# Attention's value products over four query tiles instead of two

## What is computed

```python
def attend(qblk):
    sc = jnp.einsum('bqkgd,bskd->bkgqs', qblk, k).astype(jnp.float32) * scale
    p = jax.nn.softmax(sc, axis=-1).astype(v.dtype)
    return jnp.einsum('bkgqs,bskd->bqkgd', p, v)
# y_b = attention * silu(g_b);  y = concat([y_a, y_b]);  out = y @ w_out
```

## Time and profile before

| | |
|---|---|
| median of 3 runs | 2314.97 us (2313.32 to 2316.97) |
| the profiled execution | 2311.51 us, of which the span of the trace is 2309.7 us |
| PE busy | 2269.6 us, 98% of the span |
| PEld busy | 1921.3 us, 83% |
| DVE busy | 1077.2 us, 47% |
| ACT busy | 888.3 us, 38% |
| POOL busy | 274.0 us, 12% |
| DMA | 61 GB/s over the span |
| granted tensor clock | 0.999 of full speed |

### The profile page before, as it was taken

The page is one execution under the profiler, slowest core; times in us unless marked ns, Lnnn a source line. Parts: engine busy times, 40 slices in busy tenths (PEclk is TensorE's granted clock), DMA queues, the critical chain, the costliest instruction groups (busy, mean ns, idle before and its releaser), DMA issues.

```text
span 2309.7 us, 28550 instructions
## 1 busy us (share of the span) xinstructions
PE 2269.6 (98%) x11640; PEld 1921.3 (83%) x11640; DVE 1077.2 (47%) x1439; ACT 888.3 (38%) x1426; POOL 274.0 (12%) x276
## 2 busy tenths in 40 slices
PE   7999999999999999999999999998999999999998
PEld 7887799988988779998788898887888888888887
DVE  4323399954433259983624252326344344342343
ACT  5122477744322257773434142323222222222232
POOL 0097200000029600000013020000000000000000
PEclk9999999999999999999999999999999999999999
DMA  6111000033311000003411101322111111124232
GB/s 202 37 55 37 1 1 1 1 137 111 92 55 55 18 1 1 1 8 121 146 60 37 64 19 37 111 73 85 53 54 47 43 54 43 47 95 150 92 127 73
DMA packets 104210, 141.48 MB, mean 61 GB/s; under 512 B 11670, under 2 KB 65094, under 8 KB 104102
## 3 DMA queue, kind: packets, MB, share of 16 engines
q1 hardware_dynamic: 104102, 139.97, 18.3%
HBM read 123.18 MB, written 16.78 MB: 61 GB/s over the span
## 4 chain that ended last, share of the span: by engine, by line
PE 94%; DVE 3%; ACT 1%; issue 1%; DMA 0%; SPq 0%; DVEq 0%; ACTq 0%
PE ps L199 24%; PE ps L201 24%; PE ps L200 24%; PE ps L970 5%; PE ps L985 3%; PE ps L986 3%; PE ps L957 2%; PE ps L958 2%; PE ps L934 1%; PE ps L228 1%; PE ps L275 1%; PE ps L921 1%; PE ps L1949 1%; PE ps L671 1%; DVE hT_lo L290 1%
## 5 line engine op out<-in xcount | busy, mean ns | idle before, releaser
L199 PE MATMUL ps<-w_hi,hT_hi 128*128 128x512 f32 (+1 forms) x1760 | 678.9, 386 | 1.8 <-DVE hT_lo L238 1.4
L201 PE MATMUL ps<-w_hi,hT_lo 128*128 128x512 f32 (+1 forms) x1760 | 672.7, 382 | 0.0
L200 PE MATMUL ps<-w_lo,hT_hi 128*128 128x512 f32 (+1 forms) x1760 | 672.3, 382 | 0.0
L183 DVE TENSOR_TENSOR w_lo<-w_raw,w_hi 128x2048 fp32r<-128x2048 f32 x89 | 207.7, 2334 | 542.1 <-ACT w_hi L167 539.6
L199 PEld LDWEIGHTS ps<-w_hi,hT_hi 128*128 128x128 f32 x1760 | 332.0, 189 | 65.7 <-DVE hT_lo L238 1.9
L201 PEld LDWEIGHTS ps<-w_hi,hT_lo 128*128 128x128 f32 x1760 | 331.9, 189 | 64.3
L200 PEld LDWEIGHTS ps<-w_lo,hT_hi 128*128 128x128 f32 x1760 | 332.0, 189 | 62.6 <-issue 0.5
L199 PE MATMUL ps<-hT_hi,w_hi 128*128 128x512 f32 x832 | 324.2, 390 | 5.0 <-DVE X L2519 2.7
L167 ACT ACTIVATE w_hi<-w_raw 128x2048 fp32r<-128x2048 f32 x71 | 135.9, 1914 | 502.2 <-PE ps L201 502.2
L201 PE MATMUL ps<-hT_hi,w_lo 128*128 128x512 f32 x832 | 323.7, 389 | 0.0
L200 PE MATMUL ps<-hT_lo,w_hi 128*128 128x512 f32 x832 | 323.7, 389 | 0.0
(11 more groups left out here) (203 smaller groups left out, 2365.0 us busy)
## 6 DMA issues: line engine op xcount, KB each, us to landing
w_raw<-in_ffn_w_up SPq DMA_DIRECT2D x44, 512.0 KB, 4.8
w_raw<-in_ffn_w_down SPq DMA_DIRECT2D x22, 1024.0 KB, 4.9
w_raw<-in_w_in SPq DMA_DIRECT2D x21, 1024.0 KB, 5.1
x_mid<-X SPq DMA_DIRECT2D x24, 512.0 KB, 2.7
w_raw<-in_gla_w_in SPq DMA_DIRECT2D x12, 1024.0 KB, 5.2
X<-in_x SPq DMA_DIRECT2D x16, 512.0 KB, 6.9
w_raw<-in_w_out SPq DMA_DIRECT2D x8, 1024.0 KB, 7.0
X<-x_mid SPq DMA_DIRECT2D x16, 512.0 KB, 7.2
```

The lines of the kernel that those rows point to most:

```text
L183: engine.tensor_tensor(self.p.w_lo[:, slot, 0:size], self.p.w_raw[:, slot, 0:size], plane(self.p.w_hi[:, slot, 0:size]), ALU.subtract).the ...
L199: nc.tensor.matmul(out, a_hi, b_hi, start=first, stop=False)
L200: nc.tensor.matmul(out, a_hi, b_lo, start=False, stop=False)
L201: return nc.tensor.matmul(out, a_lo, b_hi, start=False, stop=last)
```

## The change

A constant `QUAD = 4` takes the place of the group size 2.

- `values` works on groups of four items: 512 columns in a matmul, and a group's 16 matmuls are spread over four iterations, four in each. Two groups of four items are kept, so `PT_hi` and `PT_lo` double in size and now cover the whole of `hT_hi` and `hT_lo`.
- Values of group g are made in iterations 4g+6 to 4g+9 (before, of a group of two, 2g+4 and 2g+5). The first value product thus comes two iterations later, and the last one two iterations later.
- `OT` holds 512 columns, and is copied every fourth iteration (n mod 4 = 1); `turn_o` turns four tiles back, every fourth iteration (n mod 4 = 3), starting at 11. DVE's line 1146 then works on four tiles in that iteration.
- The turns of `ya` move from iterations 64 to 67 to iterations 66 to 69.

```diff
-        self.PT_hi = prog.at("PT_hi", [P, 2, TT, 2 * P], 16, F32R)
-        self.PT_lo = prog.at("PT_lo", [P, 2, TT, 2 * P], 48, F32R)
+        self.PT_hi = prog.at("PT_hi", [P, 2, TT, QUAD * P], 0, F32R)
+        self.PT_lo = prog.at("PT_lo", [P, 2, TT, QUAD * P], 32, F32R)
...
-        for j in range(2):
+        for j in range(QUAD):
             mm = self.p.nc.tensor.matmul(self.out_cols(g, j), self.OT[:, g % 2, j * P:(j + 1) * P],
                                          self.pair_ident[:], start=True, stop=True)
...
-                pe.wait_ge(self.pt_lo, 4 * g + 4)
-            for k in range(part * (TT // 2), (part + 1) * (TT // 2)):
+                pe.wait_ge(self.pt_lo, 2 * QUAD * (g + 1))
+            for k in range(part * (TT // QUAD), (part + 1) * (TT // QUAD)):
                 v = self.VS[:, head // (H_B // KV), k, :]
-                nc.tensor.matmul(prog.ps[:, 7, 0:256], v, self.PT_hi[:, g % 2, k, :], start=(k == 0), stop=False)
-                mm = nc.tensor.matmul(prog.ps[:, 7, 0:256], v, self.PT_lo[:, g % 2, k, :], start=False,
+                nc.tensor.matmul(prog.ps[:, 7, :], v, self.PT_hi[:, g % 2, k, :], start=(k == 0), stop=False)
+                mm = nc.tensor.matmul(prog.ps[:, 7, :], v, self.PT_lo[:, g % 2, k, :], start=False,
                                       stop=(k == TT - 1))
-            if part == 1:
+            if part == QUAD - 1:
                 mm.then_inc(self.ot_ready, 1)
...
-            if n % 2 == 1 and 7 <= n < NT + 5:
-                self.turn_o(pe, (n - 7) // 2, n)
-            if 4 <= n < NT + 4:
-                values(n // 2 - 2, n % 2)
-            if NT <= n < NT + 4:
-                if n == NT:
+            if n % QUAD == 3 and 11 <= n < NT + 7:
+                self.turn_o(pe, (n - 11) // QUAD, n)
+            if 6 <= n < NT + 6:
+                values((n - 6) // QUAD, (n - 6) % QUAD)
+            if NT + 2 <= n < NT + 6:
+                if n == NT + 2:
                     pe.wait_ge(self.inp.ga_used, TT)
                     pe.wait_ge(self.exp_done, NT)
-                for g in range(2 * (n - NT), 2 * (n - NT) + 2):
+                for g in range(2 * (n - NT - 2), 2 * (n - NT - 2) + 2):
                     self.ya.pe(pe, g, ya_src)
             if self.turns_head(n):
-                self.turn_head(pe, KV + n // TT + 1, n % TT // 4, max(0, (n - 6) // 2))
+                self.turn_head(pe, KV + n // TT + 1, n % TT // 4, max(0, (n - 7) // QUAD))
...
-            if n % 2 == 1 and 5 <= n < NT + 5:
-                g = (n - 5) // 2
+            if n % QUAD == 1 and 9 <= n < NT + 9:
+                g = (n - 9) // QUAD
                 act.wait_ge(self.ot_ready, g + 1)
...
-            if n % 2 == 1 and n >= 7:
-                g = (n - 7) // 2
+            if n % QUAD == 3 and n >= 11:
+                g = (n - 11) // QUAD
                 dve.wait_ge(self.o_ready, g + 1)
-                dve.wait_ge(self.inv_done, 2 * g + 2)
-                for j in range(2):
-                    m = 2 * g + j
+                dve.wait_ge(self.inv_done, QUAD * (g + 1))
+                for j in range(QUAD):
+                    m = QUAD * g + j
```

More of the change, by code:

```diff
@@ L830, in pool @@
                                     ).then_inc(self.ga_used, 1)
+QUAD = 4
 class Attention:
@@ L850, in __init__ @@
         self.pair_ident = prog.at("pair_ident", [P, HD], kb + 92.75)
-        self.PT_hi = prog.at("PT_hi", [P, 2, TT, 2 * P], 16, F32R)
-        self.PT_lo = prog.at("PT_lo", [P, 2, TT, 2 * P], 48, F32R)
+        self.PT_hi = prog.at("PT_hi", [P, 2, TT, QUAD * P], 0, F32R)
+        self.PT_lo = prog.at("PT_lo", [P, 2, TT, QUAD * P], 32, F32R)
         self.PR = [prog.at(f"PR{i}", [P, SEQ], kb_) for i, kb_ in
                    enumerate((64 + other, 68 + other, 80 + other))]
-        self.OT = prog.at("OT", [P, 2, 2 * P], 84 + other)
+        self.OT = prog.at("OT", [P, 2, QUAD * P], 84 + other)
         self.VS = prog.at("VS", [P, KV, TT, P], 96 + other, F32R)
@@ L890, in pt_of @@
     def pt_of(self, PT, m, half):
-        return PT[:, m // 2 % 2, 4 * half:4 * half + 4, m % 2 * P:(m % 2 + 1) * P]
+        return PT[:, m // QUAD % 2, 4 * half:4 * half + 4, m % QUAD * P:(m % QUAD + 1) * P]
     def out_cols(self, g, j):
-        c = g % 2 * P + j * HD
+        c = g % 2 * QUAD * HD + j * HD
         return self.p.ps[:, 6, c:c + HD]
@@ L918, in turn_head @@
         if outs:
-            pe.wait_ge(self.o_done, 2 * outs)
+            pe.wait_ge(self.o_done, QUAD * outs)
         for j in range(4):
@@ L928, in turn_o @@
         if g >= 1:
-            pe.wait_ge(self.o_done, 2 * g)
+            pe.wait_ge(self.o_done, QUAD * g)
         pe.wait_ge(self.lo_done, 2 * (KV + 1) + sum(self.turns_head(m) for m in range(n)))
@@ L938, in last_output @@
     def last_output(self, pe):
-        self.turn_o(pe, self.NT // 2 - 1, self.NT + 5)
+        self.turn_o(pe, self.NT // QUAD - 1, self.NT + 7)
     def pe(self, pe):
@@ L974, in values @@
         def values(g, part):
-            head = 2 * g // TT
+            head = QUAD * g // TT
             if part == 0:
@@ L1040, in act @@
                 m = n - 2
-                if m >= 4 and m % 2 == 0:
-                    act.wait_ge(self.ot_ready, m // 2 - 1)
+                if m >= 2 * QUAD and m % QUAD == 0:
+                    act.wait_ge(self.ot_ready, m // QUAD - 1)
                 for half in range(2):
@@ L1062, in act @@
                     act.wait_ge(self.o_ready, g - 1)
-                nc.scalar.activation(self.OT[:, g % 2, :], prog.ps[:, 7, 0:256], ACT.Copy).then_inc(self.ot_taken, 1)
-            if NT <= n < NT + 4:
-                for g in range(2 * (n - NT), 2 * (n - NT) + 2):
+                nc.scalar.activation(self.OT[:, g % 2, :], prog.ps[:, 7, :], ACT.Copy).then_inc(self.ot_taken, 1)
+            if NT + 2 <= n < NT + 6:
+                for g in range(2 * (n - NT - 2), 2 * (n - NT - 2) + 2):
                     self.ya.act(act, g)
@@ L1112, in dve @@
         QKV, G = self.inp.QKV, self.inp.G
-        for n in range(NT + 6):
+        for n in range(NT + 8):
             if self.turns_head(n - 1):
@@ L1126, in dve @@
                 m = n - 2
-                if m >= 4 and m % 2 == 0:
-                    dve.wait_ge(self.ot_ready, m // 2 - 1)
+                if m >= 2 * QUAD and m % QUAD == 0:
+                    dve.wait_ge(self.ot_ready, m // QUAD - 1)
                 for half in range(2):
```

## The result

| | before | after |
|---|---|---|
| median of 22 runs | 2314.82 us | 2318.59 us (2316.51 to 2319.84) |
| ratio, after to before | | 1.0014, 95% interval 1.0008 to 1.0021 |
| the profiled execution | 2311.51 us, span 2309.7 | 2316.51 us, span 2314.8 |

The change costs 3.2 us by the ratio (1.9 to 4.9 by its interval), 3.8 by the medians. I had said -3.3, and a range to 2318 us; the time is 0.6 us above it. The change is as small as forecast, about 0.2%, but it has the other sign, and the sum was wrong by about 6.5 us.

A forecast was written before the change was run, and what follows sets the result against it. PE was taken to bound the kernel (94% of the chain), with DVE close behind in attention. The terms -3.8 - 2.2 - 3.4 + 1.4 + 4.2 + 0.5 gave -3.3 us, from 2315.0 to 2311.7 us, range 2306 to 2318.

The forecast's parts named there:

- values of 512 columns: Value products on PE: halving the matmul count saves 0.03 us a block over 128 blocks, -3.8 us.
- turned back by fours: PE's turn-back of outputs: eight instructions in a row cost 0.81 us instead of 0.88, 32 times, -2.2 us.
- wait in iteration 5 goes: Turn-back in iteration 5 of a head no longer waits for DVE's q_lo: 7 heads, 2 layers, -3.4 us.
- new wait in iteration 6: PE's transposes in iteration 6 of a head wait about 0.1 us for DVE's low parts, 14 times, +1.4 us.
- start: Two value blocks leave iterations 4 and 5, where PE waits anyway, and are paid at the end: +4.2 us.
- end: End of attention: PE waits some 0.5 us in iterations 65 and 66, older waits go; net +0.5 us.
- The reading that idle time of the first iterations belongs to DVE: First iterations of attention: PE waits for DVE's low parts, so work removed there saves nothing; behind the +4.2 us.
- The isolated formula: Value matmuls: columns over 2.4 GHz plus about 2.5 ns each, an alternative saving of 1.3 us instead of 3.8.
- The slower one: Rival: DVE takes over behind every turned head, low parts 0.5 to 0.7 us late, 2320 us; chance 0.12.
- The faster one: Rival: value products run at the wide projection's 0.227 us and no new stall appears, 2307.5 us; chance 0.32.
- The sustained 131 ns at 512 columns: Rival that stationary loads set the value matmuls' distance: 0.52 us for four, -64 us; chance 0.01, inside faster.

The follow-up runs named there:

- q_twos: The changed kernel, values still 512 columns wide, but each group's four outputs turned back two at a time in every odd iteration; 2316.85 us, ratio 1.0015 to the kernel before.
- q_heads: The changed kernel with the second half of each next head turned in iteration 6 instead of 4; 2316.81 us, ratio 1.0011 to the kernel before.
- p_lag2: The kernel before, still groups of two, but four groups kept and values, turn-back and ya two iterations later; 2319.95 us, ratio 1.0023.

## Why the prediction was wrong, point by point

| term, both layers | forecast | measured | from |
|---|---|---|---|
| values of 512 columns | -3.8 | -3.7 | q_twos against before, 0.029 x 128 |
| turned back by fours | -2.2 | 0 | q_twos against after, 0.45 and -0.44 |
| wait in iteration 5 goes | -3.4 | -2.9 | 12 x 0.24, distance in 5 |
| new wait in iteration 6 | +1.4 | +3.2 | 12 x 0.27, q_twos and q_heads |
| start | +4.2 | +4.2 | first values, p_lag2 |
| end | +0.5 | +2.1 | the rest of 2 x 1.46; the starts at the end give 2.2 |
| sum | -3.3 | +2.9 | attentions of both layers |

Two terms were right to 0.1 us: the width, and the start, which was the largest. The old wait had the right size, 0.24 us, and the wrong count: I read 28 entries as seven heads with two waits in two layers. They are six heads, and four entries from the ends; that the numbers matched was chance. The reading that idle time of the first iterations belongs to DVE, and that values taken out of them come back whole at the end, held in every kernel with the longer lag and the heads turned in 2 and 4 (first values at 17.90 or 17.91 us). The isolated formula that I had quoted from the Trainium skill ("TensorE: Matmul & The Clock Gate", "Back-to-back issue gap") gave 1.3 us for the width; the measured 3.7 sides with the rows.

*The turn-back.* This is the largest step that failed: "Eight in a row should cost 0.44 + 0.37 = 0.81". I took the distance of 0.37 from the first of four to the next matmul for the price of four more instructions. The switch in front of them is real, 0.07 to 0.08 us, but the second four take 0.44 and not 0.37, so eight cost 0.89 and nothing is saved; q_twos shows that four cost 0.44 wherever they are put. A neighbour in the trace of before could have told me. Timeline of PE there:

```profile
287.41 0.60 PE L921 MATMUL ps<-ident,TWICE 128*128 128x128 f32 x4
287.77 0.48 PE L957 MATMUL ps<-KT_st,QT_hi 128*128 128x512 f32 x1
...
291.54 1.06 PE L970 MATMUL ps<-ident,PR 128*128 128x128 f32 x8
292.35 0.36 PE L985 MATMUL ps<-PT_hi,VS 128*128 128x256 f32 x1
```

Four transposes take 0.36 us to the next start, and eight take 0.81, so there, too, the second four take 0.45 and not 0.36.

*The new wait.* The mechanism was right and the place was right. The size, 0.1 us each, was off by a factor of nearly three, because I measured the slack at the matmul. I compared the second low part with the start of the fifth transpose. The instructions that wait are the loads of the first and of the fifth, which start ahead of their matmuls. Timeline of PEld in the kernel before, at the earlier trace rows:

```profile
442.40 1.02 PEld L970 LDWEIGHTS ps<-ident,PR 128*128 128x128 f32 x8
```

The load starts 0.23 us ahead of the matmul at 442.63. The first low part was done at about 441.13 + 0.68 = 441.81, and in the changed kernel the load starts 0.11 us behind the end of the low part (440.64 to 440.75). That leaves 442.40 - 441.81 - 0.11 = 0.48 us of slack, not 0.63. PE came 0.71 us earlier, so an estimate of the delay is 0.23 us, and the load was 0.20 late. This row was there to be read. It would not have given the cost by itself: the 0.27 us arise in three places behind that load, as shown above.

*The end.* The wait for the low parts that I forecast came in iteration 65, at 0.43 us. In 66 it was another: I had named ACT's copy among the things that cost nothing, "because scores and transposes, 1.7 us, stand before it on PE". At the end there are no scores. The copy of 0.60 us was in the open, 0.88 us of PE's time with what surrounds it. I also priced what DVE does before `ya`'s last low parts at nothing; it was 0.27 us.

*The rivals.* The slower one, DVE taking over behind every turned head, did happen at that place, at 0.27 us and not 0.6; q_heads confirms the place and rules out ACT's copy of 512 columns. The faster one is out: the values run at 0.23 us, like the scores, and the stationary loads were never the limit: half of them are gone and a block is 0.03 us shorter. The sustained 131 ns at 512 columns that the Trainium skill states in the same section is nowhere in these traces; the values stand 230 ns apart.

What stays open is 0.3 us of the 3.2 outside the attentions, which is less than the interval, and, in the new wait, how its 0.27 us divide between the two loads, and how much of it is ACT's high part of the turned head and how much DVE's `q_lo`, which q_heads moved together.

## What to carry to other kernels

Take the slack of a wait at the instruction that carries it, which on PE is here the load of the stationary tile, 0.23 us ahead of the matmul that the eye follows. Count the waits of a trace one by one before you give them a formula. When a pipeline gets a longer lag, price both ends with their own neighbours: what covered a copy in the steady state may be missing behind the last item. And before making groups larger to spare waits, look whether the waiting instruction can stand behind its neighbour: moving two lines gave 6.7 us here, while the wider groups cost 3.2.

## What the runs showed of the hardware

A wait can cost PE time without any idle time on PE in the profile: in iteration 6 PE has no gap, PEld has 0.25 us of "issue", the first matmul is on time, and the iteration is 0.27 us longer. The tile of the probabilities makes this plain. What its instructions waited for in the changed kernel:

```profile
  issue: 11.2, 20
  DVE PT_lo L1134: 6.7, 6
```

Twelve of the 20 "issue" entries, 0.25 to 0.29 us each, are the loads of iteration 6 in six heads of two layers; q_twos, which has no wait there, shows the same DVE row and 8.3 us in 10. In a sum of PE's own idle time they would not be seen. A matmul with 64 float32 columns costs as much of PE's time as a transpose with 128: from the first start to the next matmul, eight of the first take 0.81 us (456.42 to 457.23) and eight of the second 0.79 (452.84 to 453.63).
